# PEER experts of the last two prompt tiles from one pass over both whole expert tables, with dense gate weights

## The reference, cut to what matters

```
q = (t @ wq).reshape(blk, 8, 128)
s1 = einsum(q[..., :64], subkeys[:, 0]); s2 = einsum(q[..., 64:], subkeys[:, 1])   # 128 keys each
v1, i1 = top_k(s1, 16); v2, i2 = top_k(s2, 16)
cand = v1[..., :, None] + v2[..., None, :]        # 256 candidates a head
sc, pos = top_k(cand, 16); e = i1[pos // 16] * 128 + i2[pos % 16]
g = softmax(sc)
a = gelu(einsum('td,thkd->thk', t, u[e]))
out = einsum('thk,thkd->td', g * a, v[e])
```

## Time and profile before

| | |
|---|---|
| median of 3 runs | 1834.46 us (1833.58 to 1840.53) |
| the profiled execution: span | 1831.0 us |
| busy: TensorE, VectorE, ScalarE, GpSimd | 69%, 71%, 32%, 29% of the span |
| moved by DMA | 696.47 MB, 570.53 of them by the software queue of the gathers |
| first gather issued, last dot product started | 225.5 us, 1822.4 us |

### The profile page before, as it was taken

One profiled execution on the slowest core, in us unless ns is written; L12 is line 12 of the kernel. 1 busy time (PEld: TensorE's weight loads), 2 busy tenths in 40 slices (PEclk: granted clock), 3 DMA queues, 4 the chain that ended last, 5 costly groups with the idle time before them and its releaser, 6 DMA issues.

```text
span 1831.0 us, 26290 instructions
## 1 busy us (share of the span) xinstructions
PE 1256.7 (69%) x8990; PEld 693.1 (38%) x8990; DVE 1307.8 (71%) x3842; ACT 580.0 (32%) x2009; POOL 522.6 (29%) x569
## 2 busy tenths in 40 slices
PE   8989746678778565788877485889878543434353
PEld 3666612344444222455445132556536111111111
DVE  5561495888766577898767667898757768686754
ACT  2331223424323233334422333334423222222222
POOL 0100032333322323332323322322323333333332
PEclk9999859778798778788898587887997555555555
DMA  6325499999999999999999999998999999999997
GB/s 263 94 99 174 149 426 408 403 425 425 421 424 421 422 421 401 396 425 398 424 423 421 425 382 404 424 413 330 421 423 419 425 427 426 426 426 426 426 422 306
DMA packets 119380, 696.47 MB, mean 380 GB/s; under 512 B 17983, under 2 KB 21118, under 8 KB 49102
## 3 DMA queue, kind: packets, MB, share of 16 engines
q0 software_dynamic: 78848, 570.53, 74.7%
q1 hardware_dynamic: 36686, 121.83, 17.6%
q10 hardware_dynamic: 3712, 2.43, 0.4%
HBM read 691.65 MB, written 3.02 MB: 379 GB/s over the span
## 4 chain that ended last, share of the span: by engine, by line
DMA 37%; PE 27%; DVE 22%; issue 5%; ACT 4%; POOL 1%; ACTq 0%; DVEq 0%; POOLq 0%
DMA rows<-in_peer_uv,index 28%; DVE rows L2349 9%; PE ps_v L1600 6%; PE ps_f L1420 4%; PE ps_f L1470 3%; PE ps_f L1449 3%; DMA wch<-in_w_row 3%; PE ps_f L1214 3%; DMA wch<-in_w_out 2%; PE ps_h L1580 2%; DMA wch<-in_peer_wq 2%; PE ps_f L1435 1%; DVE score L2074 1%; DMA wch<-in_w_ukv 1%; PE ps_f L1298 1%
## 5 line engine op out<-in xcount | busy, mean ns | idle before, releaser
L1191 POOL DMA_INDIRECT rows<-in_peer_uv,index x544 | 512.7, 943 | 1211.4 <-PE ps_v L1600 1010.4
L2349 DVE CUSTOM_DVE_ANT_0 rows<-rows,ps_h 128x1024 f32<-128x1024 f32 x544 | 657.5, 1220 | 271.7 <-DMA rows<-in_peer_uv,index 228.7
L1600 PE MATMUL ps_v<-rows,diag 128*32 128x256 f32 x4352 | 434.2, 515 | 462.4 <-ACT diag L1910 462.1
L1600 PEld LDWEIGHTS ps_v<-rows,diag 128*32 128x32 f32 x4352 | 125.9, 133 | 719.2 <-ACT diag L1910 612.2
L1901 ACT ACTIVATE tan<-arg 128x2 f32<-128x2 f32 x272 | 55.4, 204 | 784.4 <-DVE arg L2359 765.4
L1904 ACT ACTIVATE weight<-tan,lead 128x1 f32<-128x1 f32 x544 | 180.8, 379 | 9.1
L1910 ACT ACTIVATE diag<-sel,weight 128x32 f32<-128x32 f32 x544 | 140.7, 305 | 0.0
L1420 PEld LDWEIGHTS ps_f<-bufh,wch 128*128 128x128 f32 x768 | 114.4, 233 | 22.0 <-issue 19.6
L1420 PE MATMUL ps_f<-bufh,wch 128*128 128x128 f32 x768 | 121.3, 323 | 0.0
L1214 PE MATMUL ps_f<-wch,bufh 128*128 128x512 f32 (+1 forms) x192 | 80.4, 559 | 18.3 <-DMA wch<-in_w_row 18.0
L1449 PE MATMUL ps_f<-wch,bufb 128*128 128x512 f32 x96 | 53.1, 693 | 18.4 <-DMA wch<-in_w_out 18.4
(11 more groups left out here) (359 smaller groups left out, 1675.8 us busy)
## 6 DMA issues: line engine op xcount, KB each, us to landing
wch<-in_w_gate SPq DMA_DIRECT2D x60, 512.0 KB, 8.1
wch<-in_w_row SPq DMA_DIRECT2D x36, 512.0 KB, 11.3
wch<-in_w_o SPq DMA_DIRECT2D x32, 512.0 KB, 7.8
wch<-in_w_out SPq DMA_DIRECT2D x32, 512.0 KB, 10.1
wch<-in_peer_wq SPq DMA_DIRECT2D x32, 512.0 KB, 10.6
rows<-in_peer_uv,index POOLq DMA_INDIRECT x544, 13.8
w_tok<-in_w_tok SPq DMA_DIRECT2D x4, 1640.0 KB, 13.7
wch<-in_w_uq SPq DMA_DIRECT2D x6, 384.0 KB, 4.9
```

Of the source, the lines that this page charges most:

```text
L1191: pool.indirect_dma_start(rows[c % RING][:, :, :].rearrange("p a d -> p (a d)"), None, io.peer_uv[:, :], at).then_inc(s_uv[c % RING], 16)
L1600: ins = nc.tensor.matmul(ps_v[GROUP * a:GROUP * (a + 1), :], diag[:, c % DRING, :], rows[c % RING][:, 1, QD * a:QD * (a + 1)], start=False ...
L2349: v.tensor_tensor_reduce(out=u, in0=u, in1=ps_h[:, :], scale=1.0, scalar=0.0, op0=ALU.mult, op1=ALU.add, accum_out=dots[:, c % KEEP:c % KE ...
```

## The change

Tiles i = 3 and 4 (prompt tiles 2 and 3, 256 tokens, `DENSE`) are no longer gathered. Their `choose` leaves the picks as three transposed tables: expert row index, expert column index and gate weight of each of 128 slots, for 256 tokens. From these the dense gate weights G[j, i, token] are built: for each token, one product of a one-hot matrix of j (GpSimd, 128x128) with a weighted one-hot matrix of i (VectorE, 128x64; in two halves of i). Then one pass runs over all 128 rows i of both tables: `inner` computes the dot products of 128 experts with 256 tokens, ScalarE and VectorE apply gelu and G, and `outer` adds the product with the value rows into four PSUM banks.

The columns fall from 544 to 288 (`NCOL = NG * SG`, NG = 9). The 351 ticks of passes 1 to 3 run in columns 0 to 223 (74 or 75 columns a pass), the choices of blocks 1 to 4 in columns 2 to 45 and of 5 to 8 in 75 to 118 (one part a column), of 9 to 12 in 150 to 173 (two parts a column), and of the last four in 224 to 239 (three parts a column). From column 241 on, 33 steps of `dense` run in the last 47 columns: the builds of the first half. The second half's 32 builds run beside the first 32 of 66 steps of the pass, which starts after the last column. `rows` has 8 buffers, `xb` three. The 128 + 128 loads of 512 KB of the two tables go out on SP, with three buffers for each table. `peer_ut` is a second, transposed copy of `peer_u`, laid out on the host.

The diff, cut to its core:

```diff
-NCOL = NB * SG
-RING = 9
+DENSE = (3, 4)
+NG = sum(i not in DENSE for i, _ in BLOCKS)
+NCOL = NG * SG
+RING = 8
+NSLOT = 6
+XB = {0: 0, 1: 1, 2: 2, 3: 0, 4: 1}
...
+AHEAD = 4
+TW = len(DENSE) * P
+HALVES = 2
+NI = NKEY // HALVES
+NLOW = 18
+HOT = 4
+BUILDS = TW // (2 * HOT)
+PAIRS = NKEY // 2
+EDGE = PAIRS // HALVES
+NSTREAM = 3
...
+    done = lambda k: ticks_through(NP - 1) * min(k, FRONT_COLS) // FRONT_COLS
+    return done(b + 1) - done(b)
...
+        rate = (0, 1, 1, 2, 3)[i]
+        if i > 1:
+            at = max(at, front_end(i - 1) + 1)
+        for part in range(PARTS):
+            found.setdefault(at + part // rate, []).append((n, part))
+        at += -(-PARTS // rate)
...
+def dense_at(b):
+
+    done = lambda k: (BUILDS + 1) * max(0, k - DENSE_COL) // (NCOL - DENSE_COL)
+    return done(b + 1) - done(b) if b < NCOL else 0
...
+            def load_u(e):
+                if e >= NSTREAM:
+                    sp.wait_ge(s_ux.sem, s_ux.upto(e - NSTREAM + 1))
+                sp.dma_start(u_in[e % NSTREAM][:, :], io.peer_ut[e, :, :]).then_inc(s_u[e % NSTREAM].sem, 16)
+
+            def load_v(e):
+                if e >= NSTREAM:
+                    sp.wait_ge(s_vx.sem, s_vx.upto(e - NSTREAM + 1))
+                sp.dma_start(v_in[e % NSTREAM][:, :],
+                             io.peer_uv[NKEY * e:NKEY * (e + 1), D:2 * D]).then_inc(s_v[e % NSTREAM].sem, 16)
...
+            def hots_j(n):
+                if n == 0:
+                    pool.wait_ge(s_slot.sem, s_slot.upto(NB - NG))
+                    pool.wait_ge(s_row, 1)
+                for b in range(2):
+                    r, at = 2 * n + b, 2 * HOT * (n % BUILDS) + HOT * b
+                    if r >= 2:
+                        pool.wait_ge(s_built, r - 1)
+                    for q in range(HOT):
+                        ins = nc.gpsimd.tensor_scalar(hot_j[:, r % 2, q, :], row_i[:, :], slot_j[:, at + q:at + q + 1], None,
+                                                      ALU.is_equal)
+                    ins.then_inc(s_hotj.sem, 1)
...
+                for _ in range(dense_at(c - AHEAD)):
+                    next(after)
...
+            def build(n):
+                if n == BUILDS:
+                    pe.wait_ge(s_dot, NCOL)
+                depth = 4 if n < BUILDS else 2
+                if n % BUILDS >= depth:
+                    pe.wait_ge(s_kept, n - depth + 1)
+                for b in range(2):
+                    r = 2 * n + b
+                    pe.wait_ge(s_hot, r + 1)
+                    pe.wait_ge(s_hotj.sem, s_hotj.upto(r + 1))
+                    for q in range(HOT):
+                        ins = nc.tensor.matmul(build_at(n)[:, HOT * b + q, :], hot_j[:, r % 2, q, :], hot_i[:, r % 2, q, :],
+                                               start=True, stop=True)
+                    ins.then_inc(s_built, 1)
+
+            def inner(n):
+                if n == 0:
+                    pe.wait_ge(s_both, 1)
+                else:
+                    pe.wait_ge(s_act.sem, s_act.upto(n))
+                for a in range(2):
+                    e = 2 * n + a
+                    pe.wait_ge(s_u[e % NSTREAM].sem, s_u[e % NSTREAM].upto(16 * (e // NSTREAM + 1)))
+                    w = u_in[e % NSTREAM][:, :].rearrange("p (c k) -> p c k", c=DC)
+                    for k in range(DC):
+                        ins = nc.tensor.matmul(ps_f[:, 4, TW * a:TW * (a + 1)], w[:, k, :], both[:, k, :],
+                                               start=(k == 0), stop=(k == DC - 1))
+                    ins.then_inc(s_ux.sem, 1)
+
+            def outer(n):
+                pe.wait_ge(s_made.sem, s_made.upto(n + 1))
+                for a in range(2):
+                    e = 2 * n + a
+                    pe.wait_ge(s_v[e % NSTREAM].sem, s_v[e % NSTREAM].upto(16 * (e // NSTREAM + 1)))
+                    first, final = e == 0, e == NKEY - 1
+                    for t in range(len(DENSE)):
+                        for c in range(2):
+                            ins = nc.tensor.matmul(ps_f[:, 2 * t + c, :], act_x[:, n % 3, a, P * t:P * (t + 1)],
+                                                   v_in[e % NSTREAM][:, 512 * c:512 * (c + 1)], start=first, stop=final)
+                    ins.then_inc(s_vx.sem, 1)
...
+                for n in range(BUILDS):
+                    build(n)
+                    yield
+                for q in range(PAIRS + 2):
+                    if q < PAIRS:
+                        inner(q)
+                    if q >= 2:
+                        outer(q - 2)
+                    if q < BUILDS:
+                        build(BUILDS + q)
...
+            def take(n):
+                act.wait_ge(s_ux.sem, s_ux.upto(2 * (n + 1)))
+                if n >= 3:
+                    act.wait_ge(s_vx.sem, s_vx.upto(2 * (n - 2)))
+                nc.scalar.copy(act_x[:, n % 3, :, :].rearrange("p a t -> p (a t)"), ps_f[:, 4, :]).then_inc(s_act.sem, 1)
+
+            def bend(n):
+                act.wait_ge(s_cubed.sem, s_cubed.upto(n + 1))
+                e = act_e[:, n % 2, :, :]
+                nc.scalar.activation(e, e, ACT.Tanh, scale=TANH).then_inc(s_tanh.sem, 1)
...
+            def hots(n):
+                half, t = n // BUILDS, 2 * HOT * (n % BUILDS)
+                if n == 0:
+                    dve.wait_ge(s_row, 1)
+                    dve.wait_ge(s_both, 1)
+                for b in range(2):
+                    r, at = 2 * n + b, t + HOT * b
+                    if r >= 2:
+                        dve.wait_ge(s_built, r - 1)
+                    for q in range(HOT):
+                        ins = v.tensor_scalar(hot_i[:, r % 2, q, :], row_i[:, NI * half:NI * (half + 1)],
+                                              slot_i[:, at + q:at + q + 1], slot_w[:, at + q:at + q + 1],
+                                              ALU.is_equal, ALU.mult)
+                    ins.then_inc(s_hot, 1)
+
+            def cubed(n):
+                x, e = act_x[:, n % 3, :, :], act_e[:, n % 2, :, :]
+                dve.wait_ge(s_act.sem, s_act.upto(n + 1))
+                if n >= 2:
+                    dve.wait_ge(s_made.sem, s_made.upto(n - 1))
+                step(v.scalar_tensor_tensor(out=e, in0=x, scalar=CUBE, in1=x, op0=ALU.mult, op1=ALU.mult), s_step)
+                v.scalar_tensor_tensor(out=e, in0=e, scalar=1.0, in1=x, op0=ALU.add, op1=ALU.mult).then_inc(s_cubed.sem, 1)
+
+            def gated_in(n):
+                x = act_x[:, n % 3, :, :]
+                if n % EDGE == 0:
+                    dve.wait_ge(s_kept, BUILDS * (n // EDGE + 1))
+                step(v.tensor_tensor(x, x, chosen(n), ALU.mult), s_step)
+
+            def finish(n):
+                x, e = act_x[:, n % 3, :, :], act_e[:, n % 2, :, :]
+                dve.wait_ge(s_tanh.sem, s_tanh.upto(n + 1))
```

More of the change, by code:

```diff
@@ new lines, in dense, with fronts @@
+            def dense():
+                yield
+                for n in range(BUILDS):
+                    build(n)
+                    yield
+                for q in range(PAIRS + 2):
[5 more added lines that the diff above has]
+                        build(BUILDS + q)
+                    yield
+            def fronts():
+                for p in range(1, NP):
+                    yield from front(p)
@@ L1617, in _ @@
                     n = b // SG
-                    if b % SG == SG - 1 and n + 1 < NB:
+                    if b % SG == SG - 1 and n + 1 < NG:
                         spread(n + 1)
+                for _ in range(dense_at(b)):
+                    next(after)
+            for _ in after:
+                pass
         @block.scalar
@@ new lines, in dense @@
+            def dense():
+                yield
+                for n in range(BUILDS):
+                    hots(n)
+                    yield
+                for q in range(PAIRS + 2):
+                    if q < PAIRS:
+                        cubed(q)
+                        gated_in(q)
+                    if 1 <= q <= PAIRS:
+                        finish(q - 1)
+                    if q < BUILDS:
+                        hots(BUILDS + q)
+                    yield
+                gather_sums()
@@ L2372, in _ @@
                 first_choose(h)
[L2373 to L2376 removed]
+            ahead, after = fronts(), dense()
+            for b in range(NCOL + LAG):
+                k = b % SG
                 if b < NCOL and k:
                     dot(b)
[L2379 removed]
+                if 2 <= b <= NCOL and b % 2 == 0:
                     arguments(b - 2)
@@ L2385, in _ @@
                         dot(b)
-                    if n + 1 < NB and k % 2 == 0 and 1 <= k // 2 <= PARTS:
-                        choose(n + 1, k // 2 - 1)
+                    for n, part_no in choices_at(b):
+                        choose(n, part_no)
+                for _ in range(dense_at(b)):
+                    next(after)
+            for _ in after:
+                pass
 class Names:
```

243 lines of the change are left out of this document (195 added, 48 removed).

## The result

The changed kernel takes **2525.62 us** (median of 4 runs, 2518.68 to 2534.03) against 1835.58 us of the kernel before beside it: 1.375 times as long, 95% interval 1.371 to 1.379. The forecast was 2333 us with a range up to 2450: the direction was right, the size 193 us too small. The profiled execution spans 2524.6 us.

A forecast was written before the change was run, and what follows sets the result against it. Bytes were taken to bound the kernel before from 226 us on, TensorE the new dense part. Start 230, columns 1133, last mixes 5 and dense part 962 gave a 2330 us span, 2333 with launch; range 2225 to 2450.

The forecast's parts named there:

- The bound of the dense part: Pass over the tables after the last column: TensorE sets the time at full clock, 883 us, 962 with extras.
- Rival 1: `inner` and `outer`: TensorE's pass hides under the bytes, kernel faster at 1765 us; chance 1%.
- rival 4: Pass over the tables: the clock falls, 883 us more, kernel 3216 us; chance 2%.
- rival 5: Dense tiles: the change does not do what it says, for instance their gathers remain; chance under 1%.
- the term of the last 47 columns: Last 47 columns with 32 builds: four limits close together (DMA 117, VectorE 106, TensorE 99, GpSimd 116) give 130 us.
- Rival 2: Last 47 columns: GpSimd binds, one-hot at 0.94 us, 285 us instead of 130, kernel 2488 us; chance 9%.
- Two-deep handoffs: Last 47 columns: handoffs of the one-hots, with four close limits, bring the stretch to 130 us.
- VectorE's `hot_i` at 0.16 us: Builds: each of VectorE's 8 one-hots of 64 columns takes 0.16 us.
- the passes: Passes 1 to 3, columns 0 to 223: 287, 287 and 315 us, plus 26 us as 3%.
- the sum of the largest: Columns: the busiest engine's time in each stretch, added up, 1107 us; with 3% on the passes, 1133.
- the ceiling: All columns: 1225 us, if an eighth of the second-busiest's share comes on top in every stretch.
- Rival 3: Squeezed passes: they overlap almost perfectly, columns 1010 us instead of 1133, kernel 2210 us; chance 6%.

The follow-up runs named there:

- run 4: Changed kernel with GpSimd's one-hots one column earlier relative to its gathers (AHEAD 3 for 4): 2500.71 us.
- run 1: Changed kernel with all 33 steps of builds moved from columns 241 to 287 to the last column: 2551.25 us.
- run 2: Changed kernel with GpSimd's one-hots made by VectorE, four tokens to an instruction: 2464.61 us.
- run 3: Changed kernel with GpSimd waiting for one mix more before each gather, as with seven row buffers: 2604.02 us.
- run 7: Changed kernel with each dot product over 256 of its 1024 elements, the rest left out: 2435.49 us.
- run 9: Changed kernel with only the upper 16 bits of both operands in passes 1 to 3's streamed-weight products: 2544.49 us.
- run 13: Kernel with one-hots on VectorE, choices spread evenly and upper-16-bit dense products, its dense part's one-hots moved ahead of the gelu: 1890.16 us.

## Why the prediction was wrong in size and right in direction

- **The bound of the dense part: right, and by its parts.** Two instructions a product and two cycles a column, in gapless work at full clock, gave 962 us, and 962.1 came. The median distance from start to start was 0.429 us for 512 columns and 0.216 for 256 (forecast 0.430 and 0.216); a step took 15.6 us in the first 32 and 13.8 after them (forecast 15.7 and 13.8). Rival 1 (the pass under the bytes) is out, and so is rival 4: the clock row shows 1.00. The trace has 288 dots, so rival 5 is out too. The Trainium skill (TensorE: Matmul & The Clock Gate, Back-to-back issue gap) states a spacing of 131 ns for N=512, and the prediction's estimate from it put this part under 400 us; the trace doesn't agree, with 429 ns in float32.
- **The failed step is the term of the last 47 columns, 130 us where 222.7 came.** Three of its four limits were priced too low.
  - GpSimd, "47 x 0.936 + 256 x 0.283 = 116". The one-hot took 0.599 us: its nearest row was of the same shape, but another operation (an affine select without a scalar from memory). Price 0.60 gives 200 us, and run 4 measured 199.6 once the order was eased. Rival 2 named this very place and both ends, 0.283 and 0.94, with 9%; the truth lay between.
  - TensorE, "38 + 61" = 99. It was busy 166 us, since the stretch ran at half clock, as the earlier trace rows had it (0.51) for the columns of the kernel before. The builds were priced at full clock, 1.9 us each, and took 3.95 in run 1. So at that clock 130 would have failed at GpSimd's 0.283 too: in run 2, without GpSimd's one-hots, TensorE was still busy for 153 us.
  - VectorE, "65 + 41" = 106. It was busy 147.5 us, its one-hots 91.7 of them.
- **"Two-deep handoffs"**, some 14 us in that stretch, were 23 us (run 4) and reacted sharply, +71 us for one mix more (run 3). The prediction named the list ("a gather now stands behind 8 one-hot operations") and gave it no price; it was the reverse that cost, one-hots behind a gather's wait.
- **VectorE's `hot_i` at 0.16 us** from start to start was 0.22, and 0.37 of busy time each beside GpSimd's. In the dense part that hid under TensorE, as forecast, and it counted only in the columns.
- **The second failed term, the passes: 915 forecast with the 3%, 987 measured.** The busy sums per stretch were right to a few us (173 forecast for VectorE in 75 to 118, 175.8 measured). What failed is "the sum of the largest" plus 3%: the surcharge was taken from the kernel before, where DMA was full and bounded everything. It was 98 of 889 us, 11%, and 90 of the 98 lie in the columns with choices (555 for 465), 8 in the others (432 for 424). In the former VectorE was 83 to 86% busy and not the "above 90%" forecast, and TensorE waited 144 us for diagonals. Shorter dots gave 66 us back there (run 7). Why VectorE is not full in these columns stays open: no run moves the arguments of the tanh ahead of the choices' parts. So does TensorE's share, since the clock spoilt run 9.
- **Either error alone stays in the range.** With 84 us more for GpSimd's price the whole comes to 2417 us, with 72 more for the passes to 2405; the range to 2450 lacked the two together. All columns took 1306.6 us, where the ceiling was put at 1225, and the last dot started at 1550.5 us, past the 1480 that the prediction had named as the proof of a wrong working. Rival 3, passes that overlap almost perfectly, is out by the same numbers.
- **"Eight buffers in place of nine cost nothing"**: one fewer still cost 7 us in the passes, hardly more than equal kernels differ by; right there, and not tried in the other direction.
- **The start** was put at 230 us, near the first gather (231.3 in the changed kernel), but the columns count from the first dot, 12.6 us later: a slip of bookkeeping. Small ones of 9 and 7 us stand in the table. Two readings slipped without effect: the DMA row reaches 9 in the sixth slice, and DMA in the first part of pass 3 comes to 81 us and not 84.

## What to carry to other kernels

When work is taken off a resource that was full, the next ones stand close together, and the sum of the largest in each stretch is a floor, not an estimate. Here 19% came on top where VectorE took a choice beside everything else and 2% elsewhere, where 3% had done while DMA was full. An operation that no row of the trace shows in its very form (operation, scalar from memory, engine) deserves both its bounds in the sum, not the nearest shape. A price belongs to the granted clock of the stretch in which it will be paid. And before engines are blamed for a slow step, read their fixed lists: a wait holds up all that stands behind it, and moving independent work ahead of a wait gave 23 us in one place and some 187 in another without changing any work.

## What the runs showed of the hardware that I had not expected

- GpSimd's `tensor_scalar` with `is_equal` and a scalar from memory, 128x128 float32, took 0.599 us on average against 0.283 for the affine select of the same shape.
- VectorE's 128x64 one-hot was 0.484 us long on average in the columns in which GpSimd makes its own, and 0.318 in the same columns once those had moved to VectorE. Sorted by what GpSimd was doing, in the changed kernel's trace: the 344 that met none of its instructions took 0.310 us (0.305 to 0.320); the 98 that lay inside its one-hots took 0.694 on average, with a median of 0.894, about the sum of one of each. GpSimd's own took 0.60 us either way. So it was VectorE that was held up; why some of the 98 took only 0.303 isn't shown.
- Halving the instructions of some products in stretches with gaps came with a lower granted clock (0.82 to 0.59), so that 16 to 18% fewer instructions in the windows gave no time back (run 9). Closing gaps by moving one-hots came with a higher one (0.72 to 0.99, run 13). In run 2 the last columns had TensorE busy for 94% of the time and still a granted clock of 0.53.
- A bfloat16 view of step 2 on float32 data halved the instruction count of a product, and each instruction took about half the time: a median of 0.226 us from start to start for 512 columns and 0.113 for 256 in run 13, where float32 takes two instructions of 0.429 and 0.216.
